# First-layer attention scores as three products of 64 rows, in the two row halves of TensorE in turn

## What is computed

```python
def even_layer(...):
    qa, ka, va, ga, qs, ks, vs, gs = split_cols(x @ w_in, EVEN_SPLITS)
    qa = qa.reshape(bsz, L, A_HEADS, 2, A_DH)      # 4 heads, 2 maps, 64
    ...
    s = jnp.einsum('bqhmd,bkhmd->bhmqk', qb, ka) * (A_DH ** -0.5)
    ...
    w = p[:, :, 0] - lam * p[:, :, 1]              # softmax of map 0 less that of map 1
    ...
    qs = qs.reshape(bsz, L, B_HEADS, B_DH)         # 8 heads, 64
    z = jnp.einsum('bqhd,bkhd->bhqk', qb, ks) * (B_DH ** -0.5)
    log_skip = jnp.where(earlier, jax.nn.log_sigmoid(-z), 0.0)
    ...
```

## Time and profile before

| | us |
|---|---|
| median of 3 runs | 1390.32 (1390.18 to 1390.37) |
| profiled execution | 1394.38, its span 1392.6 |
| TensorE matmul busy | 1342.1 (96% of the span), 8600 matmuls |
| TensorE weight load busy | 1244.0 (89%) |
| VectorE busy | 871.5 (63%) |
| ScalarE busy | 551.3 (40%) |
| GpSimd busy | 488.4 (35%) |

### The profile page before, as it was taken

One profiled execution on the slowest core, in us unless ns is written; L12 is line 12 of the kernel. 1 busy time (PEld: TensorE's weight loads), 2 busy tenths in 40 slices (PEclk: granted clock), 3 DMA queues, 4 the chain that ended last, 5 costly groups with the idle time before them and its releaser, 6 DMA issues.

```text
span 1392.6 us, 22854 instructions
## 1 busy us (share of the span) xinstructions
PE 1342.1 (96%) x8600; PEld 1244.0 (89%) x8600; DVE 871.5 (63%) x1969; ACT 551.3 (40%) x1290; POOL 488.4 (35%) x458
## 2 busy tenths in 40 slices
PE   8999999999899999998999999998999999999997
PEld 7999998989799998987788999997998989988886
DVE  5675768594477757759556323645667667677465
ACT  3443546363545535345111012623454545545200
POOL 3313232123224242347433223553324233244531
PEclk9999999999999999999999999999999999999999
DMA  6000101101010111212333201221020111104242
GB/s 213 32 31 31 46 23 40 32 31 46 32 39 24 35 43 37 70 41 74 104 131 121 107 31 61 77 87 57 28 65 24 46 40 61 61 16 165 91 160 76
DMA packets 47501, 88.09 MB, mean 63 GB/s; under 512 B 4496, under 2 KB 30224, under 8 KB 47264
## 3 DMA queue, kind: packets, MB, share of 16 engines
q1 hardware_dynamic: 44944, 78.25, 17.1%
q10 hardware_dynamic: 2448, 8.39, 1.6%
HBM read 66.64 MB, written 19.98 MB: 62 GB/s over the span
## 4 chain that ended last, share of the span: by engine, by line
PE 56%; DVE 4%; POOL 3%; ACT 2%; issue 1%; DMA 0%; DVEq 0%; SPq 0%; POOLq 0%; ACTq 0%
PE bank L1898 24%; PE bank L2047 13%; PE bank L1965 7%; PE bank L2021 7%; PE bank L1991 4%; POOL big L1068 1%; POOL wsp L1025 1%; ACT rtmp L1303 1%; PE bank L1937 1%; POOL wsp L1024 1%; PE bank L2069 1%; POOL pb L1183 0%; PE bank L1969 0%; DVE pb L1680 0%; ACT pb L1375 0%
## 5 line engine op out<-in xcount | busy, mean ns | idle before, releaser
L1898 PE MATMUL bank<-big,wsp 128*128 128x344 f32 (+2 forms) x3024 | 569.6, 330 | 13.7 <-DVE big L1510 4.9
L1898 PEld LDWEIGHTS bank<-big,wsp 128*128 128x128 f32 x3024 | 481.0, 189 | 22.5 <-DVE qh L1574 6.0
L1024 POOL TENSOR_SCALAR wsp<-wraw 128x1024 fp32r<-128x1024 f32 (+3 forms) x92 | 87.7, 953 | 554.3 <-PE bank L1898 435.4
L1695 DVE TENSOR_TENSOR ring<-bank,ring 128x256 fp32r<-128x256 f32 (+3 forms) x292 | 157.5, 555 | 83.1 <-ACT ring L1385 80.7
L2047 PE MATMUL bank<-big,wsp 128*128 128x512 f32 x816 | 198.2, 399 | 2.2 <-POOL big L1068 2.2
L1385 ACT ACTIVATE ring<-bank 128x256 fp32r<-128x256 f32 (+3 forms) x292 | 139.6, 494 | 147.8 <-PE bank L1991 99.5
L2021 PE MATMUL bank<-ring,vtok 128*128 128x256 f32 (+2 forms) x1276 | 185.9, 280 | 3.5 <-DVE ot L1722 2.9
L1025 POOL TENSOR_TENSOR wsp<-wraw,wsp 128x1024 fp32r<-128x1024 f32 (+3 forms) x92 | 184.4, 2004 | 7.7
L2047 PEld LDWEIGHTS bank<-big,wsp 128*128 128x128 f32 x816 | 152.5, 189 | 36.7 <-issue 1.5
L2021 PEld LDWEIGHTS bank<-ring,vtok 128*128 128x128 f32 (+1 forms) x1276 | 171.7, 189 | 10.7 <-issue 5.5
L1898 PE MATMUL bank<-h1t,wsp 128*128 128x344 f32 (+2 forms) x1080 | 173.8, 321 | 1.1 <-DVE lraw L1556 1.1
(11 more groups left out here) (130 smaller groups left out, 1454.9 us busy)
## 6 DMA issues: line engine op xcount, KB each, us to landing
wraw<-in_w SPq DMA_DIRECT2D x47, 512.0 KB, 3.5
wraw<-y_scratch SPq DMA_DIRECT2D x17, 448.0 KB, 3.7
woraw<-in_wo SPq DMA_DIRECT2D x12, 512.0 KB, 5.5
y_scratch<-ot SPq DMA_DIRECT2D x40, 128.0 KB, 1.7
xres<-in_x SPq DMA_DIRECT2D x8, 512.0 KB, 4.5
h_scratch<-res ACTq DMA_DIRECT2D x8, 512.0 KB, 2.7
gate_scratch<-gtmp SPq DMA_DIRECT2D x8, 512.0 KB, 2.9
gate<-gate_scratch SPq DMA_DIRECT2D x8, 512.0 KB, 3.6
```

Source lines behind the costliest of these rows:

```text
L1024: pool.wait_ge(S["pool_step"], tick(nc.gpsimd.tensor_scalar(hi, raw, 1.0, 1.0, ALU.mult, ALU.mult)))
L1695: V.tensor_tensor(R[0:rows, r % NRING, 1, 0:w], bank[T_BANK[t]][0:rows, 0:w], lo_hi(R[0:rows, r % NRING, 0, 0:w]), ALU.subtract).then_inc( ...
L1898: ins = mm(dst, wsp[:, SLOT[kind, u], a, k, :], rhs[:, b, k0 + k, c0:c0 + w], start=(k == 0 and a == 0 and b == 0), stop=last)
```

## The change

- Keys and queries are stored as they come out of the projection: `kst[:, u % 2, 0]` and `qst[:, u % 2, 0]` hold the high parts of both maps or heads, one in partitions 0 to 63, the other in 64 to 127; index 1 holds the low parts. ACT and DVE write each with one instruction of 128 rows where it was two of 64. The POOL copies of layer 0 are gone, and `qst` has two buffers.
- A score step of layer 0 is made for a pair of chunks at once: maps 0 and 1 of a kind-A head, or heads 0 and 1 of a kind-B unit. Six matmuls of 64 rows (hi*hi, hi*lo, lo*hi), in turn from partitions 0 to 63 into one bank and from 64 to 127 into the next. The masks of both follow.
- Before the pair, TensorE waits for both banks. For kind B the steps of the two heads alternate. `weave` plans a pair at three matmuls and 60 ns, and 114 ns for two masks.
- The scores of layer 1 keep their products.

```diff
+def pair_of(s):
+    _, t, m, c = s
+    return [("S", t, 0, c), ("S", t, 1, c)] if kind_of(t) == "A" else [("S", t, 0, c), ("S", t + 1, 0, c)]
...
+PAIR = 3
...
-        L.put("pe", "S", s, pe_ns(w) * (5 if layer else 2) + 57 * masked, after, 170)
+        if layer:
+            L.put("pe", "S", s, pe_ns(w) * 5 + 57 * masked, after, 170)
+        elif is_first(s):
+            after += [freed(s_steps[n - 2])] if n >= 2 else []
+            L.put("pe", "S", s, pe_ns(w) * PAIR + 114 * masked + 60, after, 170)
+        else:
+            L.put("pe", "S", s, 0, [], 170)
...
-            if kind in ("q0", "qn", "qr") and u >= 1:
+            if kind in ("qn", "qr") and u >= 1:
                 end = [last_score(u - 1, c)]
+            if kind == "q0" and u >= 2:
+                end = [last_score(u - 2, c)]
...
-                if s[0] == "P" and s[1] in ("q0", "qr"):
+                if s[0] == "P" and s[1] == "qr":
                     copy_queries(s)
...
                 elif kind == "q0":
-                    for m in range(2):
-                        ins = A(qst[0:64, m, 0, cc], src[64 * m:64 * m + 64, 0:w], ACT.Copy, scale=q_scale(u))
+                    ins = A(qst[:, u % 2, 0, cc], src[:, 0:w], ACT.Copy, scale=q_scale(u))
...
                 if kind == "k0":
-                    for m in range(2):
-                        ins = V.tensor_tensor(kst[64:128, u % 2, m, cc], src[64 * m:64 * m + 64, 0:w],
-                                              lo_hi(kst[0:64, u % 2, m, cc]), ALU.subtract)
+                    ins = V.tensor_tensor(kst[:, u % 2, 1, cc], src[:, 0:w], lo_hi(kst[:, u % 2, 0, cc]), ALU.subtract)
...
             def scores(t, m, c):
+
+                s = ("S", t, m, c)
                 g, i, slot = TSTEPS[t]
                 layer, kind, u, head, _ = GROUPS[g]
+                if layer == 0 and not is_first(s):
+                    return
...
+                mine = [S_CHUNK[x[1:]] for x in ([s] if layer else pair_of(s))]
+                for b in mine:
+                    if S_BEFORE[b] is not None:
+                        pe.wait_ge(S["s_free_" + S_OWNER[S_BEFORE[b]]], S_FREED[S_BEFORE[b]])
...
-                    j = m if kind == "A" else head
-                    prods = [(qst[:, j, a, qc], kst[:, u % 2, j, c0:c0 + w]) for a in (0, 1)]
-                for k, (l, r) in enumerate(prods):
-                    ins = mm(dst, l, r, start=(k == 0), stop=(k == len(prods) - 1 and not masked))
+                    halves = [slice(64 * j, 64 * j + 64) for j in range(2)]
+                    prods = [(b, qst[h, u % 2, a, qc], kst[h, u % 2, b_, kc])
+                             for a, b_ in ((0, 0), (0, 1), (1, 0)) for b, h in zip(mine, halves)]
+                done = {}
+                for k, (b, l, r) in enumerate(prods):
+                    done[b] = mm(bank[S_BANK[b]][:, 0:w], l, r, start=(k < len(mine)),
+                                 stop=(k >= len(prods) - len(mine) and not masked))
```

More of the change, by code:

```diff
@@ L145, in make_groups @@
     for g, group in enumerate(groups):
-        tsteps += [(g, i, slot) for slot, i in enumerate(group[4])]
+        if group[1] == "B":
+            if group[3] == 0:
+                tsteps += [(g + m, i, slot) for slot, i in enumerate(group[4]) for m in range(2)]
+        else:
+            tsteps += [(g, i, slot) for slot, i in enumerate(group[4])]
     return groups, tsteps
@@ L173, in score_steps, with score_order, is_first @@
 def score_steps(g):
-    return [("S", t, m, c) for t in GROUP_STEPS[g] for m in range(maps_of(GROUPS[g][1]))
-            for c in range(len(score_chunks(TSTEPS[t][1])))]
+    return [("S", t, m, c) for t in GROUP_STEPS[g] for c in range(len(score_chunks(TSTEPS[t][1])))
+            for m in range(maps_of(GROUPS[g][1]))]
+def score_order(groups):
+    out = []
+    for g in groups:
+        if GROUPS[g][1] == "B":
+            if GROUPS[g][3] == 0:
+                out += between(score_steps(g), score_steps(g + 1))
+        else:
+            out += score_steps(g)
+    return out
+def pair_of(s):
+    _, t, m, c = s
+    return [("S", t, 0, c), ("S", t, 1, c)] if kind_of(t) == "A" else [("S", t, 0, c), ("S", t + 1, 0, c)]
+def is_first(s):
+    return s[2] == 0 if kind_of(s[1]) == "A" else GROUPS[TSTEPS[s[1]][0]][3] == 0
 def queries(u, chunks):
@@ L363, in weave @@
             cq = chunk_of(i)
-            copied = ("P", "qr", u - u % 2, cq) if layer else ("P", "q0", u, cq)
-            after += [("pool", copied)] if copied in within else []
-            after += [evacuated(("P", "qn", u, cq))] if layer else []
+            copied = ("P", "qr", u - u % 2, cq)
+            after += [("pool", copied)] if layer and copied in within else []
+            after += [evacuated(("P", "qn" if layer else "q0", u, cq))]
         masked = c == len(chunks) - 1 and not (i == META_Q and kind == "A")
-        L.put("pe", "S", s, pe_ns(w) * (5 if layer else 2) + 57 * masked, after, 170)
+        if layer:
[3 more added lines that the diff above has]
+            L.put("pe", "S", s, pe_ns(w) * PAIR + 114 * masked + 60, after, 170)
+        else:
+            L.put("pe", "S", s, 0, [], 170)
         if kind == "B":
@@ L1948, in scores @@
                     cq = chunk_of(i)
+                    pe.wait_ge(S["proj_evac"], PTURN["P", "qn" if layer else "q0", u, cq] + 1)
                     if layer:
[L1950 to L1954, removed]
@@ L1966, in scores @@
                 if masked:
                     dw = META if i == META_Q else 128 if kind == "B" else CHUNK
-                    ins = mm(bank[S_BANK[b]][:, w - dw:w], eyebf[:, :],
-                             mask[:, 1, 0:dw] if kind == "B" else mask[:, 0, 128 - dw:128], start=False, stop=True)
-                ins.then_inc(S["s_done"], 1)
+                    for b in mine:
+                        done[b] = mm(bank[S_BANK[b]][:, w - dw:w], eyebf[:, :],
+                                     mask[:, 1, 0:dw] if kind == "B" else mask[:, 0, 128 - dw:128], start=False, stop=True)
@@ L1973, in turn_weights @@
+                for b in mine:
+                    done[b].then_inc(S["s_done"], 1)
             def turn_weights(g, k):
```

30 lines of the change are left out of this document (13 added, 17 removed).

## The result

| | us |
|---|---|
| before, median of 6 runs beside it | 1390.51 |
| after, median of 6 runs | 1394.97 (1394.49 to 1395.71) |
| ratio | 1.0028, interval 1.0015 to 1.0041 |
| profiled execution after | 1394.6, its span 1392.8 |

The change costs 3.9 us by the ratio (0.28%), 4.5 us by the two medians. The direction was forecast, and the time lies in the range, but the forecast was +10.1, some two and a half times what was measured. A reader who sets the two first profiles side by side finds spans of 1392.6 and 1392.8 and might conclude that nothing changed.

The account below looks back on a forecast made before the run. The prediction took TensorE's own stream (busy 96%) as the bound: 55.4 slots + 22.8 entries + 10.4 exits - 73.8 old slots = +14.8, less 4.7 waits, +10.1 us; median 1390.3 to 1400.4, range 1374 to 1432.

Parts of the forecast that it names:

- Slots: Layer 0's 120 score pairs: six half-row matmuls take three slots instead of four, 73.8 to 55.4 us, a gain of 18.4.
- the loads bind: Score pairs: weight loads of both halves queue one after the other at 0.11 us; +37.5 us, 1427.8, chance 0.26.
- Borders: Going into and out of half-row runs: 120 entries at 0.19 us, 22.8, and 52 unmasked exits at 0.20, 10.4 us.
- masks at zero: The 68 masked exits from half-row runs cost nothing more than the masks before: 0.25 us against 0.24 a pair.
- the terms for a masked exit: Behind a half-row run: 0.09 us to empty, 0.04 small load, two mask slots of 0.04, 0.08 load after; given as 0.25.
- rival of cheap borders: At pair borders the array only empties and loads stay hidden, so the kernel is faster: -14.2 us, 1376.1, chance 0.22.
- Waits for copies: TensorE's six waits for POOL copies of layer 0's queries, 4.7 us, all counted as gained; bounds 0 and 4.7.
- its bound of 5: Pairs waiting for two of three banks: taken as 0 us, bounds 0 to 5 us.
- full granted clock throughout: Reading of the profile before: TensorE busy 96% of the span, always at full clock; no clock term in the sum.
- I cost this at nothing: the cover is TensorE's full stream: Layer 0's evictions and copies: some 22 us less on ACT, 25 on DVE, 40 on POOL, counted as no gain.
- The sum was carried over to the median: The +10.1 us was added to the profiled execution, 1394.4, and to the median, 1390.3, which stood 4.1 lower.

Follow-up runs that it names:

- same_half: Changed kernel, but both products of each couple read partitions 0 to 63, still into two banks in turn; 1446.2 us, one run.
- extra_border: Changed kernel with one more full-row product of 16 zero columns between first and second couple of every layer 0 pair; 1429.1 us, one run.
- evict_64: Changed kernel, but ACT and DVE write layer 0's keys and queries with two 64-row instructions each, order unchanged; 1414.5 us, ratio 1.0174.
- copies_unplanned: Changed kernel with POOL copies of queries kept and TensorE waiting for them, but given no time in the plan; 1449.3 us, ratio 1.0418.
- the plans with other prices: Changed kernel, a pair planned at 0, 120, 150, 190 or 270 ns over three matmuls; 1401.7, 1395.8, 1390.9, 1398.1, 1403.8 us.
- evictions, planned: Changed kernel with 64-row evictions of keys and queries, their longer durations given to the plan as before the change; 1398.9 us, ratio 1.0057.
- pairs alone: Kernel before with score chunks made in pairs and both masks side by side, still full-row products, copies and one buffer; 1393.1 us, ratio 1.0010.

## Why the prediction was right and wrong

- **Slots.** Forecast -18.4, measured 73.7 to 55.3. Right: the halves run together, and banks alone don't do it (same_half). Loads of the two halves go together too, so the rival "the loads bind" fell; both loads of a couple start within the row's 0.01 us:

```profile
42.15 0.19 PEld L1999 LDWEIGHTS bank<-kst,qst 64*128 64x128 f32 x2 [0.21 <-issue]
```

- **Borders.** Forecast 33.2 with masks at zero, measured 41.0 less the 5.8 of masks: 35.2. Right in mechanism and within 2 us, read off the 16-row instructions. The closeness is partly luck: the terms for a masked exit, 0.09, 0.04, twice 0.04 and 0.08, make 0.29 us and not 0.25, so with its own terms the forecast is 3.4 us higher (68 x 0.05). The rival of cheap borders fell by extra_border.
- **Waits for copies.** Forecast -4.7. All six are gone, but three of some 1.3 to 1.5 us for two banks came (4.0 us; forecast 0, its bound of 5 held), and one of 5.7 us at the end of the attention. The term left out the clock. The prediction read the earlier trace rows as "the full granted clock throughout", but a 9 there is 90% or more, and the earlier trace rows has 0.99 for 340 to 640 us: that is the stretch at 1.2 GHz behind the copies' longest wait, 1.7 to 2.0 us that went with it.
- **"I cost this at nothing: the cover is TensorE's full stream".** This is the step that failed, with the -4.7 beside it; and the sum had no term at all for the new order in which `weave` puts every engine's instructions. The gaps and waits of TensorE fell by 12.9 us in place of 4.7. That the work on ACT, DVE and POOL reaches TensorE is shown by evict_64 (19.5 us in the same order) and copies_unplanned (54 us in the same order of TensorE, DVE and ACT). That the order alone moves the time is shown by the plans with other prices (up to 13 us). A stream that is 96% busy on average has short places where the next instruction needs what another engine has just made, and the order sets how many.
- **What stays open.** How the 11.4 us split over the parts. Undone one by one they give 9.2 (copies), 3.9 (evictions, planned) and 0.5 (buffer), 13.6 in sum; less the 1.4 that pairs alone cost in the layout of before, 12.2. But only the run of the buffer has the order of the change, and an order alone moves the time by up to 13 us, so that this is near 11.4 may be luck. Open as well is how the 12.9 us split over shorter work, order and clock. By the same token the change's +3.9 is a property of this change with this order; what is its own is that half-row products cost 15.9 us more than full-row ones in one and the same order.
- **The median and the profile.** The sum was carried over to the median rightly, but the first profile of before held a start that was 2.7 us late, which the second profile, 0.8 us over its median, did not have.

## What to carry to other kernels

Products in row halves save a slot for a couple, but each run of them between full-row instructions pays twice, going in and coming out, for a gap of some 0.09 us and for a weight load in the open, here 0.34 us a run on average; so count borders before slots, and look for any small-row instruction in the trace that already shows their price. Where a program orders several engines by a plan, a changed cost anywhere reorders everything: an effect below the spread of neighbouring plans (here 13 us in 1395) is shown only by an experiment that keeps the order and changes one thing. And "hidden behind a full engine" needs the same test, since 23 us more on an engine that is two thirds busy in the stage, and 22 on one half busy, cost 19.5 here in an order made without them, and 3.9 once the plan knew of them. A wait of an engine can cost more than its length, too: look at the granted clock in and just behind it, in a narrow window, since the row of the page in 40 slices does not show it.

## What the runs showed that I had not expected

- Matmuls of different row halves start out of program order: with three of the first half listed before three of the second, the fourth starts 0.01 us after the first, and the time is the same (1395.5).
- Weight loads of the two halves start within 0.01 us of each other. In the same trace no two full-array float32 loads start less than 0.05 us apart, and in a stream of transposes they follow each other at 0.11.
- Different banks alone do not let two matmuls overlap (+51 us from the same half).
- TensorE's granted clock fell to 1.2 GHz for stretches in or just behind waits of one to six us (3.2 us in before, 5.7 us after, and ten stretches, 51 us, in copies_unplanned).
- A plan with the measured durations was slower than one with wrong ones, in both kernels (+5.3 and +4.5 us by the medians).
